# A transformer trunk on one core: the opening restaged (first norm tile by tile, six shift blocks on TensorE, x loaded first, the first four weight slabs worked off together)

## What is computed

```python
    c_act = jax.nn.silu(c)
        mod = c_act @ mod_w[i] + mod_b[i]
        sh1, sc1, g1, shm, scm, gm, sh2, sc2, g2 = jnp.split(mod, N_MOD, axis=-1)
        h = modulate(rmsnorm(x, ffn_norm_w[i, 0]), sh1, sc1)
        x = x + FFN_HALF * g1[:, None, :] * swiglu(h, ffn_w_gu[i, 0], ffn_w_down[i, 0])
```

## Time and profile before

| | before |
|---|---|
| median of 3 runs | 2182.48 us (2182.41 to 2184.53) |
| the profiled execution | 2180.39 us |
| its span in the profile | 2178.6 us |
| PE busy | 2093.5 us, 96% of the span |
| DVE, ACT busy | 1176.7 us (54%), 837.1 us (38%) |
| first matmul of an FFN product | 39.52 us after the span's start |

### The profile page before, as it was taken

The page is one execution under the profiler, slowest core; times in us unless marked ns, Lnnn a source line. Parts: engine busy times, 40 slices in busy tenths (PEclk is TensorE's granted clock), DMA queues, the critical chain, the costliest instruction groups (busy, mean ns, idle before and its releaser), DMA issues. The chain is left out here.

```text
span 2178.6 us, 27837 instructions
## 1 busy us (share of the span) xinstructions
PE 2093.5 (96%) x10422; PEld 1749.9 (80%) x10422; DVE 1176.7 (54%) x1835; ACT 837.1 (38%) x1296; POOL 8.0 (0%) x30
## 2 busy tenths in 40 slices
PE   4999999999999999999999999999998799999998
PEld 2888888987777778788888888888897678888887
DVE  7555566687777744555566733333256755333323
ACT  4222222476666734222222432222244634222322
POOL 0000000000000000000000000000010000000000
PEclk8999999999999999999999999999999999999999
DMA  7655466353343322555566332233322022223331
GB/s 292 223 193 192 176 223 236 111 157 102 111 132 116 111 78 88 215 194 193 178 222 235 121 102 96 96 96 100 113 78 59 0 68 88 96 96 96 105 97 68
DMA packets 83216, 291.73 MB, mean 134 GB/s; under 512 B 8896, under 2 KB 11712, under 8 KB 83008
## 3 DMA queue, kind: packets, MB, share of 16 engines
q1 hardware_dynamic: 82848, 290.49, 39.8%
q10 hardware_dynamic: 288, 0.13, 0.0%
HBM read 288.36 MB, written 2.23 MB: 133 GB/s over the span
## 5 line engine op out<-in xcount | busy, mean ns | idle before, releaser
L234 PE MATMUL bank<-h_hi,w_hi_sb 128*128 128x512 f32 (+1 forms) x1984 | 758.8, 382 | 30.7 <-DVE h_lo L375 21.0
L236 PE MATMUL bank<-h_hi,w_lo_sb 128*128 128x512 f32 (+1 forms) x1984 | 747.6, 377 | 0.0
L235 PE MATMUL bank<-h_lo,w_hi_sb 128*128 128x512 f32 (+1 forms) x1984 | 747.4, 377 | 0.0
L229 DVE TENSOR_TENSOR w_lo_sb<-raw,w_hi_sb 128x1024 fp32r<-128x1024 f32 x356 | 421.5, 1198 | 127.4 <-ACT w_hi_sb L224 122.0
L234 PEld LDWEIGHTS bank<-h_hi,w_hi_sb 128*128 128x128 f32 x1984 | 375.4, 189 | 107.6 <-issue 20.2
L236 PEld LDWEIGHTS bank<-h_hi,w_lo_sb 128*128 128x128 f32 x1984 | 375.1, 189 | 69.3
L235 PEld LDWEIGHTS bank<-h_lo,w_hi_sb 128*128 128x128 f32 x1984 | 375.7, 189 | 67.6 <-issue 1.7
L224 ACT ACTIVATE w_hi_sb<-raw 128x1024 fp32r<-128x1024 f32 x356 | 354.0, 1028 | 86.6 <-PE bank L236 84.7
L234 PE MATMUL bank<-a_hi,w_hi_sb 128*128 128x512 f32 (+1 forms) x792 | 290.1, 366 | 0.0
L236 PE MATMUL bank<-a_hi,w_lo_sb 128*128 128x512 f32 (+1 forms) x792 | 289.4, 365 | 0.0
L235 PE MATMUL bank<-a_lo,w_hi_sb 128*128 128x512 f32 (+1 forms) x792 | 289.4, 365 | 0.0
(11 more groups left out here) (204 smaller groups left out, 1675.2 us busy)
## 6 DMA issues: line engine op xcount, KB each, us to landing
raw<-w_stream SPq DMA_DIRECT2D x356, 512.0 KB, 3.9
mod_raw<-w_mod SPq DMA_DIRECT2D x144, 512.0 KB, 4.6
first_mod<-w_mod SPq DMA_DIRECT2D x16, 512.0 KB, 14.6
sums<-sums_rows SPq DMA_DIRECT2D x7, 1024.0 KB, 8.6
decays<-decay_rows SPq DMA_DIRECT2D x8, 768.0 KB, 4.7
x_trunk<-x_in SPq DMA_DIRECT2D x1, 2048.0 KB, 10.5
trunk_out<-x_trunk SPq DMA_DIRECT2D x2, 512.0 KB, 2.8
trunk_out<-x_trunk SPq DMA_DIRECT2D x4, 256.0 KB, 2.1
```

The costliest lines, as they stand in the source:

```text
L229: nc.vector.tensor_tensor(w_lo_sb[:, s, 0:width], raw[:, s, 0:width], w_hi_sb[:, s, 0:width], ALU.subtract).then_inc(w_lo, 1)
L234: nc.tensor.matmul(ps, s_hi, m_hi, start=start, stop=False)
L235: nc.tensor.matmul(ps, s_hi, m_lo, start=False, stop=False)
L236: return nc.tensor.matmul(ps, s_lo, m_hi, start=False, stop=stop)
```

## The change

What it does, in the order of the engines:

- SP issues c_row, c once more as 8 columns (`c_col`), x in two transfers of 1 MB, `cols`, and then for j = 0 to 7 block 8 + j (scale of tile j) and block j (shift of tile j), with slabs 0 and 1 behind j = 0, slab 2 behind j = 2, slab 3 behind j = 3.
- The shift columns of tiles 0 to 5 are made by PE: the six blocks hold w_mod in another layout, and `shift_tensor(j)` is 8 float32 matmuls of 128 x 128 against one column of `c_col`. DVE makes the other ten blocks (8 of scale, 2 of shift).
- DVE's work of the first norm is written out in `first_norm_vector`: it makes the columns of two tiles at a time (`collect(g)`), and puts blocks and `prep_lo` of slabs 0 to 3 between the tiles.
- PE works off slabs 0 to 3 in `first_quad`: a step of a pair of slabs (`pair_step(u, k)`, 6 matmuls) as its tile of h_lo comes, the second pair one step behind the first, and two of the shift blocks in between.
- ACT loads the table for ln ahead of the squares; slabs 0 and 1 are prepared ahead of rstd, slab 2 behind it, slab 3 after the first h_hi tile.
- The first FFN has `halved=True` now: its first turn is `first_quad` on PE and, on ACT and DVE, the order quoted above. Its other turns and all that follows are as before.

```diff
+        def first_norm_vector(dve):
+            made = [0]
...
+            def collect(g):
+                two = slice(2 * g, 2 * g + 2)
...
+                if 2 * g < MOD_TENSOR:
+                    dve.wait_ge(first_shift, 2 * g + 2)
+                    nc.vector.tensor_tensor(mod[:, M_SH1A, two], bank[(4, 5, 7)[g]][:, 0:2], b[:, M_SH1A, two],
+                                            ALU.add).then_inc(mod_step, 2)
+                    made[0] += 2
...
+            scale(0)
+            scale(1)
+            prep_lo(dve, 0, 0)
+            prep_lo(dve, 0, 1)
+            scale(2)
+            scale(3)
+            collect(0)
+            collect(1)
+            dve.wait_ge(rs_step, 2)
+            scaled(0)
+            prep_lo(dve, 0, 2)
+            rest(0)
+            scaled(1)
+            prep_lo(dve, 0, 3)
+            rest(1)
+            scaled(2)
+            scale(4)
+            rest(2)
+            scaled(3)
+            scale(5)
+            rest(3)
+            collect(2)
+            scaled(4)
+            scale(6)
+            rest(4)
+            scaled(5)
+            shift(6)
+            rest(5)
+            scale(7)
+            shift(7)
+            collect(3)
+            scaled(6)
+            scaled(7)
+            rest(6)
+            rest(7)
...
+        def shift_tensor(pe, j):
+            pe.wait_ge(first_loaded[j], 16)
+            if j == 0:
+                pe.wait_ge(c_ready, 2)
+            for k in range(DT):
+                mm = nc.tensor.matmul(shift_bank(j), first_mod[:, j, k * P:(k + 1) * P], c_col[:, k:k + 1],
+                                      start=(k == 0), stop=(k == DT - 1))
+            mm.then_inc(first_shift, 1)
...
+        def first_quad(pe):
+            def pair_step(u, k):
+                pe.wait_ge(h_lo_ready, k + 1)
...
+            for j in range(4):
+                shift_tensor(pe, j)
+            pair_step(0, 0)
+            shift_tensor(pe, 4)
+            pair_step(0, 1)
+            shift_tensor(pe, 5)
+            pair_step(0, 2)
+            pair_step(1, 0)
+            pair_step(1, 1)
+            for k in range(3, 6):
+                pair_step(0, k)
+                pair_step(1, k - 1)
+            pair_step(0, 6)
+            pair_step(1, 5)
+            pair_step(0, 7)
+            pair_step(1, 6)
+            pair_step(1, 7)
...
+                if first and k == 0:
+                    first_quad(pe)
+                    pe.wait_ge(a_ready, ONE + 1)
+                    return
...
+            for j in range(DT):
+                for m in (DT + j, j):
+                    sp.dma_start(first_mod[:, m, :], w_mod[m]).then_inc(first_loaded[m], 16)
+                for n in {0: (0, 1), 2: (2,), 3: (3,)}.get(j, ()):
+                    sp.dma_start(raw[:, n, :], w_stream[n]).then_inc(raw_loaded[n], 16)
...
-            ffn_scalar(act, 0, S_FFN0, 1, mods0, between=lambda: wdt_scalar(act))
+            ffn_scalar(act, 0, S_FFN0, 1, mods0, halved=True, between=lambda: wdt_scalar(act))
```

More of the change, by code:

```diff
@@ L67 @@
 MOD_FIRST = 2
+MOD_TENSOR = 6
 MOD_GU = GU_SLABS // 8
@@ L106, in trunk @@
         spare = sb(ctx, "spare", [P, 17])
+        c_col = sb(ctx, "c_col", [P, DT])
         cols = sb(ctx, "cols", [P, NCOLS])
@@ L538, in down_mod, with shift_bank @@
             return None if mod0 is None else mod0 + MOD_GU
+        def shift_bank(j):
+            return bank[(4, 5, 7)[j // 2]][:, j % 2:j % 2 + 1]
+        def shift_tensor(pe, j):
[9 more added lines that the diff above has]
+                pe.wait_ge(h_lo_ready, k + 1)
+                w = slice(k * P, (k + 1) * P)
+                for l in range(2 * u, 2 * u + 2):
+                    if k == 0:
+                        pe.wait_ge(w_lo, l + 1)
+                    mm = product3(bank[l][:, :], w_hi_sb[:, l, w], w_lo_sb[:, l, w], h_hi[:, k, :], h_lo[:, k, :],
+                                  k == 0, k == 7)
+                    if k == 7:
+                        mm.then_inc(slab_used, 1)
+            for j in range(4):
[15 more added lines that the diff above has]
+            pair_step(1, 7)
         def ffn_tensor(pe, k, n0, hs, st, mod0=None, halved=False):
@@ L1622, in _ @@
             dve.wait_ge(c_ready, 1)
-            for v in range(MOD_FIRST):
-                for k in range(8):
-                    mod_block(dve, v, k, first=True)
-                if v == 0:
-                    dve.wait_ge(in_loaded, 16)
-                else:
-                    prep_lo(dve, 0, 0)
-                    prep_lo(dve, 0, 1)
-                mod_collect(dve, v)
-            dve.wait_ge(mod_col, 2)
-            columns_vector(dve, 1, M_SC1A, col("nw_ffn0"))
-            norm_vector(dve, 0, 0, M_SH1A, h_hi, h_lo)
-            ffn_vector(dve, 0, S_FFN0, M_G1A, 1, mods0, 1, between=lambda: wdt_vector(dve))
+            first_norm_vector(dve)
+            ffn_vector(dve, 0, S_FFN0, M_G1A, 1, mods0, 1, halved=True, between=lambda: wdt_vector(dve))
             columns_vector(dve, 3, M_SCMA, col("nw_mix0"))
@@ L1738, in lay_out @@
     return {"w_stream": stream, "w_mod": w_mod, "w_dt": w_dt, "x_in": x_t, "c_in": np.ascontiguousarray(i["c"][0]),
+            "c_cols_in": np.ascontiguousarray(columns(i["c"][0])),
             "cols_in": np.ascontiguousarray(cols),
```

68 lines of the change are left out of this document (51 added, 17 removed).

## The result

| | before | after |
|---|---|---|
| median | 2182.48 us (2181.55 to 2184.53, 7 runs) | 2193.45 us (2189.83 to 2197.84, 7 runs) |
| the profiled execution | 2180.39 us | 2195.17 us |
| its span | 2178.6 us | 2193.3 us |
| first matmul of an FFN product | 39.52 us | 33.99 us |
| slots of slabs 0 and 1 free (t0) | 52.8 us | 63.43 us |

The account below looks back on a forecast made before the run. PE, 96% busy, bounds the kernel, so only an earlier start could gain. t0 56.7 + 22.4 put slab 6 at 79.1 against 75.35 us, 3.8 later: 2182.5 + 3.8 = 2186.3 us; range 2180 to 2193.

Parts of the forecast that it names:

- clock low for long: Rival, chance 0.25: clock returns 5.7 us into dense PE work, after shift block 5; t0 62.3, slab 6 84.7, 2191.8 us.
- the clock's return: PE's first quad: full clock back at about 36.9 us, 5.7 us after the first pair step begins at 31.2.
- E: End of `collect(1)` on DVE, where its chain of tiles starts; forecast 28.6 us.
- The clock's fall: PE in the opening: clock falls to half at about 23 us, so shift block 3 runs at half clock.
- The sums of squares: PE's sums in the opening: 9.05 us from 8.6 us, ending at 17.6 us.
- The price of a block: One shift block on PE: 1.8 us at the full clock, 3.4 us at half.
- DVE's chain from E to tile 7: DVE after `collect(1)`: tile 0 at E + 2.6, tile 3 at E + 10.6, tile 7 at E + 22.6 us.
- The second turn: From t0, DVE and the loads bound the first FFN's second turn: slab 6 starts at t0 + 22.4 us.
- Clock kept: Rival, chance 0.27: one-column products and the short hole leave full clock; E 27.0, slab 6 at 75.4, no change, 2182.5 us.
- The second turn doesn't stall: Rival, chance 0.09: loads of blocks 18 to 21 come sooner; slab 6 at t0 + 15.0, 2178.8 or 2175.2 us.
- The blocks are not what E waits for: Rival, part of "Clock kept": shift blocks on PE take 1.1 us or less; E 26.3, slab 6 at 74.7, 2181.8 us.
- a clock that is low for still longer: Case of the clock staying low beyond the rival "clock low for long"; left out of the range.

Follow-up runs that it names:

- Four blocks early: Changed kernel, with DVE doing blocks 16 to 19 before it prepares slabs 4 and 5 in the first FFN's first turn: 2189.91 us.
- two blocks early: Changed kernel, with only blocks 16 and 17 ahead of slabs 4 and 5 on DVE in the first FFN: 2186.90 us.
- products left out: Changed kernel without PE's six shift blocks (those values are not the reference's), loads kept: 2182.50 us.
- the same with blocks early: Changed kernel without PE's shift products, and the first two blocks ahead of the third pair of slabs in first and second FFN: 2169.60 us.
- four shift blocks: Changed kernel with shift blocks 4 and 5 back on DVE, and the first two blocks moved ahead in both FFNs: 2178.36 us.
- block 4 ahead and two blocks early: Changed kernel with shift block 4 right behind block 3 on PE, and the first two blocks moved ahead in both FFNs: 2177.09 us.
- block 4 ahead: Changed kernel with shift block 4 right behind block 3 on PE, before the first pair step: 2191.39 us.
- 512-column products between: Changed kernel with unused 512-column products on PE, one behind each of shift blocks 0 to 2 and three behind block 3: 2190.95 us.
- pairs in turn: Changed kernel, with PE doing all eight steps of slabs 0 and 1 before those of slabs 2 and 3: 2194.12 us.

## Why the prediction was wrong

The forecast was 2186.3 us and its range ended at 2193; the median is 2193.45. What happened is the rival "clock low for long", held at one in four, whose numbers were t0 62.3, slab 6 at 84.7, a wait of 4 us at `collect(2)` and 2191.8 us. Measured: 63.43, 87.2, 4.89 and 2193.45. The return came 3.0 us after shift block 5, though, and not the rival's 5.7; block 5 itself ended 2.9 us later than in its sum.

One thing has to be kept in mind for what follows: 63.43 and 87.2 are of one execution (2195.17 us), and the changed kernel's seven run from 2189.83 to 2197.84. "Four blocks early" and "two blocks early" have the same order on PE up to t0, and there t0 was 58.4 and 58.3. With the 23.7 us of this kernel's second turn that would put slab 6 at 82.1 and the time at 2189.2, near the lowest of the seven (an estimate; no trace of the changed kernel shows it).

**The step that failed: the clock's return.** The prediction said "By the 5.7 us of the earlier trace rows the clock returns at about 36.9". It counted 5.7 us from the first pair step, through shift block 4. The clock came back at 49.1, 15.1 us after that step began and 3.0 us after the last shift block. In the five other traces with shift blocks and no other products among the pair steps it came back between 40.6 and 48.3, which is 8.8 to 15.5 us after the first step; in all six that is 2.7 to 5.9 us after the end of a shift block. Where nothing stands between the pair steps it took 4.7 us from the first of them (products left out), 4.2 (the same with blocks early) and 5.2 (four shift blocks). So none of the six has the 5.7 us of the forecast, and the step fails in the executions with the early return too. With the same order on PE the return came at 40.7, 40.8 or 49.1 us, so how late it is isn't fixed by the order. Why shift blocks delay it stays open. Of the 6.7 us by which t0 is later than forecast, 2.8 lie in E and 3.9 behind it, nearly all of them in `collect(2)`, which waited 4.89 us where 1.2 were summed.

**The clock's fall: right in kind, too late.** "So about 23" was 21.8. The shift blocks were in hand at that time: blocks 1 to 3 went through at half rate one behind the other, and ended at 30.8. The prediction took blocks 0 to 2 at 1.8 us and only block 3 at 3.4. PE, not the transfer of block 3, was what `collect(1)` waited for. E is 31.39, 2.8 us later than 28.6. The transfers alone would have made it 1.2 (block 11 at 24.41 where 23.2 was summed); the other 1.6 are the queue of blocks. Both differ between executions. Seven traces, that of the changed kernel among them, are of kernels alike until shift block 3. In four of them the clock fell at 23.0 to 23.7 us, blocks 0 to 2 went through at the full rate, as forecast, and E was 28.5 to 29.3; in the other three it fell at 21.0 to 21.8, and E was 30.2 to 31.4. Block 11 came at 23.1 to 24.4.

**The sums of squares** ended at 19.5, not 17.6. The 9.05 us of the earlier trace rows became 9.60, and they began 1.3 us later than 8.6. The lateness of the transfers shows here already: the squares, which wait for the first half of x, began at 9.14 where 7.9 was summed. It matters only since the blocks stand behind them on PE.

**The price of a block: right.** 1.8 and 3.4 us were forecast, 1.84 and 3.41 measured. The Trainium skill, "FP8 and Floating Point Precision" (TensorE Precision Notes), has true float32 in four passes, from which the prediction worked out, with a weight load for each pass, an estimate of 3.4 us at the full clock. The traces don't agree with a load for each: three blocks take 5.42 us at the full clock (17.57 in the kernel with block 4 ahead and two blocks early), with 16 records for the eight products of a block, and the 3.41 us of a block in the changed kernel belong to the half clock.

**DVE's chain from E to tile 7: right.** Tile 0 at E + 2.5 (2.6 forecast), tile 3 at E + 9.9 (10.6), tile 7 at E + 26.2, which without the 4.9 us of `collect(2)` is 21.3 (22.6).

**The second turn: right, 1.3 us too short.** t0 + 23.7 against t0 + 22.4. PE waited 0.8 us for the multiplication (1.4 forecast) and 5.3 before slabs 6 and 7 ("together over 4 us"); 13 matmuls ran at half rate. Without the products it was t0 + 23.5, with block 4 ahead + 22.7. With two blocks early it was + 17.1 to 17.3 in three kernels; in two others PE still waited 1.8 and 3.0 us for slab 7, the clock fell again, and it was + 18.9 and + 21.5. That the early start of the first product is worth nothing, since the second turn is bound by DVE and its loads, was the prediction's main reason against a gain. The run without products (2182.50, same as before) shows it.

**The rivals.** "Clock kept" fell: no trace kept it, not with 512-column products between. "The second turn doesn't stall" fell for this kernel, with the point named for it: block 18's load was issued at 70.19, t0 + 6.8, against the t0 + 6.5 from which it would decide. "The blocks are not what E waits for" asked for 1.1 us a block or less and fell with the 1.84 us measured.

**The range.** It stopped at 2193 because "a clock that is low for still longer" was left out, and because 2191.8 was taken without a width. Against that rival's sum the trace has E 2.8 us later, 1.2 of it by the loads, and the second turn 1.3 us longer. Each is small, and all had the same sign. The 0.45 us by which 2193.45 lies beyond the range are less than the spread of the seven executions; but none of them is below 2189.83, so the forecast's own 2186.3 was not reached by any.

**Open.** The medians of four blocks early, block 4 ahead and two blocks early in the first FFN alone are 3 to 5 us above what slab 6 of their profiled executions would give (2182.5 + 4.2, 3.7 and 0.1). Other executions than the profiled one have no trace. The moment of the clock's fall differs between traces of kernels that are alike until then (21.0 to 23.7 us), and so does that of its return (40.7 to 49.1), and by them how many shift blocks and pair steps run at half rate. That this spreads the times is argued, not shown.

## What to carry to other kernels

A start that is moved forward is worth what the next bound lets through: follow it to the first place where the old and the new timeline meet again (here slab 6), and look there for a queue that is fed only as fast as its consumer counts. Price small products that are put on TensorE ahead of or among large ones at half clock, and the large ones behind them too: in the three traces with the order of the change blocks 3 and 4 ran so each time, and the clock came back 8.8 to 15.1 us after the first large product. Where work has landed and its engine has a hole, do it there: one line moved ahead in the second FFN gained 5.6 us, which no form of the restaging that makes its shift columns gave by itself.

## What the runs showed of the hardware

- One-column products with PE 100% busy didn't hold the clock: it fell 2.3 us after the last 512-column product ended (19.5 to 21.8), and in the kernel with pairs in turn at 21.0. In the kernel without them, with PE idle, it fell 5.0 us after that end. The time from the end of dense work to the fall was 2.3 to 5.4 us over the traces.
- With one 512-column product behind each of shift blocks 0 to 2 and three behind block 3 the clock fell at 25.8 us in one trace and at 27.7 in another, with the same order on PE, against 21.0 to 23.7 without them. It was kept in neither.
- The same order on PE gave a return of the clock at 40.6 and at 43.5 us, and in the order of the change at 40.7, 40.8 and 49.1 us. The Trainium skill, "TensorE: Matmul & The Clock Gate" (Part 1), says that the number of slow matmuls at a start varies from run to run of one kernel; the traces agree: before the return at 40.7 us PE had done 12 matmuls of 512 columns at half rate, before that at 49.1 us 19.
- A block of eight float32 products of 128 x 128 by one column takes 1.84 us at the full clock and 3.41 us at half: it goes with the clock almost entirely.
